# Prompt attention's two-map weights scaled, subtracted and turned by TensorE products with diagonals from ScalarE, in place of VectorE arithmetic and a transpose

## What is computed

```python
def diff_attn_prompt(q, k, v, lam):
    ...
    def block(args):
        qi, i = args
        s = jnp.einsum('bqhmd,bkhmd->bhmqk', qi, k, preferred_element_type=F32) * ATTN_SCALE
        qpos = i * Q_BLOCK + jnp.arange(Q_BLOCK)
        s = jnp.where(kpos[None, :] <= qpos[:, None], s, -jnp.inf)
        p = jax.nn.softmax(s, axis=-1)
        w = p[:, :, 0] - lam * p[:, :, 1]
        return jnp.einsum('bhqk,bkhd->bqhd', w.astype(v.dtype), v)
```

## Time and profile before

| what | value |
|---|---|
| median of 3 runs | 2125.33 us (2123.13 to 2126.2) |
| the profiled execution | 2127.41 us, its span 2125.8 us |
| mean granted clock of TensorE over the span | 0.916 |
| TensorE busy | 1877.3 us, 88% of the span |
| VectorE busy | 780.2 us, 37% |
| ScalarE busy | 722.0 us, 34% |
| GpSimd busy | 174.3 us, 8% |
| the chain that ended last | TensorE 72%, transfers 8%, SyncE's queue 5%, VectorE 4%, ScalarE 3% |

### The profile page before, as it was taken

One profiled execution on the slowest core, in us unless ns is written; L12 is line 12 of the kernel. 1 busy time (PEld: TensorE's weight loads), 2 busy tenths in 40 slices (PEclk: granted clock), 3 DMA queues, 4 the chain that ended last, 5 costly groups with the idle time before them and its releaser, 6 DMA issues.

```text
span 2125.8 us, 43188 instructions
## 1 busy us (share of the span) xinstructions
PE 1877.3 (88%) x17058; PEld 1647.2 (77%) x17058; DVE 780.2 (37%) x1200; ACT 722.0 (34%) x1056; POOL 174.3 (8%) x321
## 2 busy tenths in 40 slices
PE   4999995999999978979878988788769599999998
PEld 1647994999999978977433767677539599999997
DVE  3993333333322333156477222222223423333222
ACT  4432333333332223244333644344111333333222
POOL 2100122000000221010010000000004200000000
PEclk9899996999999988989677999999768799999999
DMA  8775321222222221212442899899851122222222
GB/s 233 261 265 177 95 86 30 79 84 84 79 68 81 82 86 50 79 50 90 133 134 90 272 393 349 322 345 381 318 186 50 35 84 79 85 83 67 82 81 72
DMA packets 245680, 302.86 MB, mean 142 GB/s; under 512 B 10451, under 2 KB 195774, under 8 KB 245438
## 3 DMA queue, kind: packets, MB, share of 16 engines
q1 hardware_dynamic: 241504, 292.14, 41.6%
q10 hardware_dynamic: 3142, 8.11, 1.1%
q0 software_dynamic: 928, 1.06, 0.2%
HBM read 293.89 MB, written 7.37 MB: 142 GB/s over the span
## 4 chain that ended last, share of the span: by engine, by line
PE 72%; DMA 8%; SPq 5%; DVE 4%; issue 4%; ACT 3%; POOL 2%; DVEq 0%; POOLq 0%; ACTq 0%
PE ps L538 54%; PE ps L464 5%; DMA kpg<-in_cache_k 4%; SPq L415 3%; PE ps L491 2%; SPq L422 2%; PE ps L778 1%; DMA vpg<-in_cache_v 1%; PE ps L829 1%; PE ps L926 1%; PE ps L815 1%; DMA xcm<-in_x_sample 1%; PE ps L684 1%; PE ps L767 1%; PE ps L677 1%
## 5 line engine op out<-in xcount | busy, mean ns | idle before, releaser
L538 PE MATMUL ps<-hr,ws 128*128 128x288 f32 x5760 | 796.7, 301 | 60.4 <-DVE hr L1838 60.4
L538 PEld LDWEIGHTS ps<-hr,ws 128*128 128x128 f32 x5760 | 787.9, 193 | 70.3 <-issue 37.4
L1832 DVE TENSOR_TENSOR ws<-raw,ws 128x1024 fp32r<-128x1024 f32 x200 | 234.8, 1175 | 715.4 <-ACT ws L1219 715.4
L1219 ACT ACTIVATE ws<-raw 128x1024 fp32r<-128x1024 f32 x200 | 201.5, 1009 | 709.6 <-PE ps L538 651.9
L538 PE MATMUL ps<-gr,ws 128*128 128x288 f32 x2112 | 281.9, 296 | 0.0
L538 PEld LDWEIGHTS ps<-gr,ws 128*128 128x128 f32 x2112 | 281.7, 189 | 0.0
L1399 ACT ACTIVATE kTs<-ps 128x512 f32<-128x512 f32 x256 | 140.0, 596 | 184.5 <-PE ps L464 184.3
L464 PE MATMUL ps<-identz,kpg 128*128 128x128 f32 x1024 | 147.3, 291 | 35.1 <-DMA kpg<-in_cache_k 33.8
L464 PEld LDWEIGHTS ps<-identz,kpg 128*128 128x128 f32 x1024 | 119.7, 149 | 59.5 <-ACT kTs L1399 29.5
L491 PE MATMUL ps<-raw,cond 128*32 128x256 f32 x896 | 87.5, 484 | 28.8 <-DMA raw<-in_w_ada_mix 23.3
L538 PE MATMUL ps<-hg,ws 128*128 128x288 f32 x768 | 104.1, 299 | 3.1 <-DVE mark L1825 3.1
(11 more groups left out here) (320 smaller groups left out, 1588.9 us busy)
## 6 DMA issues: line engine op xcount, KB each, us to landing
kpg<-in_cache_k SPq DMA_DIRECT2D x128, 512.0 KB, 5.8
vpg<-in_cache_v SPq DMA_DIRECT2D x128, 512.0 KB, 5.9
raw<-in_ffn_w SPq DMA_DIRECT2D x88, 512.0 KB, 3.8
raw<-in_w_ada_mix SPq DMA_DIRECT2D x48, 512.0 KB, 5.2
raw<-in_w_ada_ffn SPq DMA_DIRECT2D x48, 512.0 KB, 4.3
raw<-in_ffn_w SPq DMA_DIRECT2D x48, 384.0 KB, 3.3
raw<-in_w_ada_kv SPq DMA_DIRECT2D x16, 512.0 KB, 4.9
raw<-in_ssm_w_glu SPq DMA_DIRECT2D x16, 512.0 KB, 4.1
```

The costliest lines, as they stand in the source:

```text
L538: last = mm(ps[:, 4 * s + 2 * tile + h, 0:HALF], ws[:, wslot, w, k, :], src[:, k0 + k, v, h * HALF:(h + 1) * HALF], start=first, stop=(end ...
L1219: A(ws[:, w, 0, 0:nk, :].rearrange("p k n -> p (k n)"), raw[:, slot, 0:nk, :].rearrange("p k n -> p (k n)"), ACT.Copy).then_inc(slab_high, 1)
L1832: TT(f(ws[:, w, 1, 0:nk, :]), f(raw[:, slot, 0:nk, :]), f(ws[:, w, 0, 0:nk, :]).bitcast(F32), ALU.subtract).then_inc(raw_done[slot], 1)
```

## The change

VectorE's `block_weights` ends after the reciprocal and the factor of minus lambda. ScalarE gets a new step, `block_diag`, after the exponentials of the following block: it waits for w_done and writes two 128x128 diagonal matrices (the identity times the two per-query factors) into a new buffer `diag`, of two parities; semaphore d_done. TensorE's `block_weights` waits for d_done instead of w_done and makes, for each 128 keys, two matmuls that accumulate in PSUM: exponentials of map 0 turned by the first diagonal, plus those of map 1 turned by the second. These give the scaled, subtracted and turned weights in one go.

```diff
-    l01 = share("l01", [P, 2, 8], 46 * KB)
+    l01 = share("l01", [P, 2, 8], 47 * KB)
...
+    diag = share("diag", [P, 2, 2, P], 44 * KB + 512)
...
             def block_weights(h, i):
-                pe.wait_ge(w_done, h * QB + (i + 1))
+                pe.wait_ge(d_done, h * QB + (i + 1))
                 pe.wait_ge(wp_copied, h * QB + (i + 1))
                 for k in range(i + 1):
-                    last = turn(ps[:, 4 + i % 2, k * P:(k + 1) * P], e01[:, i % 2, 0, k * P:(k + 1) * P])
+                    for m in range(2):
+                        last = mm(ps[:, 4 + i % 2, k * P:(k + 1) * P], e01[:, i % 2, m, k * P:(k + 1) * P], diag[:, i % 2, m, :],
+                                  start=(m == 0), stop=(m == 1))
                 last.then_inc(wp_turned, 1)
...
+            def block_diag(h, i):
+                act.wait_ge(w_done, h * QB + (i + 1))
+                for m in range(2):
+                    done = A(diag[:, i % 2, m, :], ident, ACT.Copy, scale=l01[:, i % 2, 6 + m:7 + m])
+                done.then_inc(d_done, 1)
...
                         elif not (final and hp):
                             block_exp(h + 1, 0)
+                        block_diag(h, i)
                         if i == 1 and not (first and hp == 0):
                             head_output(h - 1)
...
             def block_weights(h, i):
 
-                w, par = (i + 1) * P, i % 2
-                l_, e0, e1 = l01[:, par], e01[:, par, 0, 0:w], e01[:, par, 1, 0:w]
+                l_ = l01[:, i % 2]
                 dve.wait_ge(e_done, h * QB + (i + 3))
                 step(REC(l_[:, 6:8], l_[:, 4:6]))
-                step(TT(l_[:, 7:8], l_[:, 7:8], neglam[:, :], ALU.mult))
-                step(TS(e1, e1, l_[:, 7:8], None, ALU.mult))
-                STT(e0, e0, l_[:, 6:7], e1, ALU.mult, ALU.add).then_inc(w_done, 1)
+                TT(l_[:, 7:8], l_[:, 7:8], neglam[:, :], ALU.mult).then_inc(w_done, 1)
```

More of the change, by code:

```diff
@@ L247, in yoco_step @@
     tri = share("tri", [P, P], 44 * KB)
+    diag = share("diag", [P, 2, 2, P], 44 * KB + 512)
+    assert 44 * KB + 512 + 4 * 4 * P <= 47 * KB
     kpg = share("kpg", [P, 4, H, P], 0)
@@ L305, in yoco_step @@
         picks_ready, sums_done, sums_root, sums_inv, spread = sems("picks_ready sums_done sums_root sums_inv spread")
-        head_in, s_full, s_max, e_done, w_done, wp_turned, wp_copied, pv_full, head_out = sems(
-            "head_in s_full s_max e_done w_done wp_turned wp_copied pv_full head_out")
+        head_in, s_full, s_max, e_done, w_done, d_done, wp_turned, wp_copied, pv_full, head_out = sems(
+            "head_in s_full s_max e_done w_done d_done wp_turned wp_copied pv_full head_out")
         k_full, v_full = [sem(f"k_full{s}") for s in range(4)], [sem(f"v_full{s}") for s in range(4)]
@@ L1981, in _ @@
             head_pair(0, first=True)
-            with step.loop(1, H // 2 - 2, 2 * QB * 5) as k:
+            with step.loop(1, H // 2 - 2, 2 * QB * 3) as k:
                 head_pair(k)
```

## The result

The changed kernel takes **2136.45 us** (median of 5 runs, 2135.32 to 2141.02) against 2125.33 in the same series (5 runs, 2119.41 to 2128.91): a ratio of 1.0062, 95% interval 1.0040 to 1.0084. It is slower by 11 us. The profiled execution took 2141.02, its span 2139.4.

A forecast was written before the change was run, and what follows sets the result against it. TensorE's ring in prompt attention, waiting for VectorE's scaled weights, was taken as the bound. A pair of heads grows from 30.5 to 33.6 us, times 3.5 pairs +11 us on 2125.3: 2136, range 2128 to 2143.

The forecast's parts named there:

- The removal: Prompt attention, VectorE: dropping L1955 (12.4 us) and L1956 (17.6 us) can by itself win at most 30 us.
- the ring: Prompt attention's chain of waits between engines over 32 blocks, returning to TensorE: 15.25 us a head, 30.5 a pair before.
- The diagonals: ScalarE, behind the next block's exponentials: two 128x128 writes cost 0.68 us a pair, bounds 0.45 and 0.81.
- The waits: TensorE's waits: 2.10 us ahead of block 2, 0.28 and 0.85 ahead of block 3, 1.14 at the second head's end.
- The walk: Step-by-step timing of two heads at full clock: 31.8 us a pair, 25.3 of work and 6.5 of waiting.
- The clock: TensorE in prompt attention: a tenth of the work at half clock in place of 30%, giving 33.6 us a pair.
- ScalarE is never late: Rival: TensorE finds each diagonal ready, leaving 25.3 us of work a pair; -18 us, 2107; chance 0.04.
- S+3.10: First head: block 3's exponentials start on ScalarE 3.10 us after S, the start of block 3's scores on TensorE.
- full clock throughout: Rival: TensorE stays at full clock because bursts are longer; 31.8 us a pair, +4.5, 2130; chance 0.21.
- The clock falls as often as now: Rival: 30% of TensorE's work stays at half clock; 37.9 us a pair, +26, 2151; chance 0.07.
- No change: Rival: diagonal writes cost 0.45 us a pair and the clock holds; 30.7 a pair of heads, 2126; chance 0.08.
- The prediction's own sign against the rule: Trace before: from 1169.43 TensorE did sixteen transposes for 3.69 us at half clock, then the clock rose to full.

The follow-up runs named there:

- e4_no_vector: Kernel before, with VectorE's scaling of map 1 and subtraction left out, TensorE turning map 0's bare exponentials: 2098.58 us.
- e9_transposes: Changed kernel with its 160 products put back to 80 transposes of map 0's exponentials, still waiting for the diagonals; scales and second map left out: 2126.23 us.
- e8_no_link: Changed kernel without ScalarE's diagonal step; TensorE's products take both maps against the identity and wait for VectorE's scales: 2109.97 us.
- e1_early: Changed kernel with VectorE's scales ahead of the next block's reduction and ScalarE's diagonals ahead of the next block's exponentials: 2110.0 us, ratio 0.9933.
- e2_products: Kernel before, with each transpose of a block of weights made twice as a full-precision product with the identity, no diagonals: 2121.06 us.

## Why the prediction was right

The forecast was 2136 in a range of 2128 to 2143; 2136.45 was measured. The mechanism held; two terms were off and cancelled, and the bound on the removal held by luck.

- **The removal.** VectorE's 30 us were called the most that the removal could win. Alone it shortens the stretch by 27.9 (e4_no_vector), but only 11.5 of that is less idle time of TensorE; 16.4 is its clock, for which the bound had no term although the prediction itself counts 5.6 us a pair of work done at half clock. That the two stayed under 30 together was luck.
- **What takes it back.** In the stretch: 114.8 before; 86.9 without VectorE's part; 115.4 with the link too (+28.5, e9_transposes); 125.6 with the products too (+10.2). "So the change removes VectorE's link of the ring and puts ScalarE's in its place, equally late, and TensorE's longer groups come on top" was the sentence; taken in this order the link eats the whole gain, and the loss that is left is the groups. The shares depend on the order in which the parts are added: with the products first (e8_no_link, 100.7) they cost 13.8 and the link 24.9.
- **The diagonals.** Priced at 0.68 a pair from L1088; the timeline shows 0.68 and 0.69, one of them 395 ns. The Trainium skill, "ScalarE: Activation LUTs", What ACT_TABLE_LOAD costs, gives 186 ns and 0.833 a column for an activation with immediate scale and bias, 93 more for an operand read from a per-partition pointer, and an overlap of 93 between neighbours: an estimate of 386 ns for one and 0.68 us for the pair, and the trace agrees.
- **The waits.** 2.10 ahead of block 2, measured 1.97; 0.28 and 0.85 ahead of block 3, measured 0.33 and 0.90 in the pair of heads at full clock; 1.14 ahead of the next head's block 0, measured 0.96. These measured waits begin when the scores ahead of them are wholly done, 0.07 us later than in the walk (0.49 in the profile for the narrowest scores, which it counts as 0.42).
- **The walk.** 31.8 us a pair at full clock. The widest reductions of the changed kernel, with the next two heads at full clock, start at

```profile
1059.09 1.22 DVE L1956 TENSOR_REDUCE l<-ps 128x2 f32<-128x1024 f32 x1
1074.81 1.22 DVE L1956 TENSOR_REDUCE l<-ps 128x2 f32<-128x1024 f32 x1
1091.35 1.22 DVE L1956 TENSOR_REDUCE l<-ps 128x2 f32<-128x1024 f32 x1
```

15.72 and 16.54, 32.26 for the pair: **0.46 short**. Nearly all of it is the groups, counted from start to start as in the walk: at full clock (e1_early's timeline) groups of 4, 8, 12 and 16 records take 0.65, 1.09, 1.54 and 1.89, or 5.17 a head where I had 4.96. My 0.14 for a group's start was a little low.
- **The clock.** A tenth of the work at half clock was to cost 1.8 a pair net. Over all seven heads the widest reductions are 117.4 us apart (1059.09 to 1176.52), 33.55 a pair, so it cost 1.3. That term was too dear by 0.5 and the walk too cheap by 0.46: the 33.6 came out right by two errors that cancel. That the clock would stay above 0.73 and between 0.85 and 0.95 held (0.87 in the window of the earlier trace rows, 1038 to 1170).
- **Not held:** that everything outside the stage stays as long as it was. In the profiles the stage began 8 us later, and what lies behind the last head's values took 6 less (951.1 against 957.1). Neither can be put down to the change: the start of the stage moves by as much between kernels that are alike up to there, and the part behind it takes 947.2 to 955.0 in the eleven other profiles, though its code is the same. That the widest reductions would be 16 to 17.5 us apart held for their mean, 16.8, and for two of the seven gaps; the others are 15.72 (three times), 17.75 and 18.99.

Of the rivals, "ScalarE is never late" had nearly the right price for a thing that needed one more edit, the order of both engines. I put 25.3 us a pair and 2107 on it; e1_early and e8_no_link, where TensorE hardly waits ahead of the products, run a pair in 26.3 and 26.4 and take 2110. I bound its condition to ScalarE's order as the diff has it (start of the exponentials at S+3.10), and there it fails. What I did not ask is what ScalarE does before S+3.10: nothing, for 2.40 us. The rival "full clock throughout" is refuted: the clock in the stretch is 0.92, and the products of block 2 at 1111.88 above run near half clock (2.81 us, granted clock 0.53, against 1.60 at full for the same group at 1062.63). "The clock falls as often as now" would have kept it near the 0.76 of before. "No change" needed a pair of diagonals in 0.45 us; it takes 0.68.

## What to carry to other kernels

Where a change puts an engine's new step into a ring, look at what that engine does right before the step: a short step that stands behind a long wait costs the ring as much as the work it replaced, and ahead of that wait it costs nothing (25 us of a 125 us stretch here), if what the step needs is made early enough too. Effects in a ring don't add: price a removal with the new link in place, since whatever is late next decides what the removal is worth. And measure a stage by its own landmarks where its start moves by more than the effect.

## What was not expected of the hardware

**In these runs the clock went with the waits and the length of the groups between them, not with the kind of instruction.** With the same 80 transposes the granted clock in the stretch was 0.92 where TensorE waited 8.7 us (e4_no_vector) and 0.76 where it waited 25.9 (e9_transposes). With 22 us of waits and four times the records it was 0.92 for products and 0.90 for transposes. The Trainium skill, "TensorE: Matmul & The Clock Gate", Part 4: PE-mode transpose, says that transposes don't engage the full clock; the runs here differ from it: with 320 transposes in the stage, 49.7 us of TensorE's time, the clock in the stretch was 0.90. No run has a stage of transposes alone. The prediction's own sign against the rule was weaker, as 4.65 us of values ended 0.7 us before its sixteen transposes.

**A wait costs more than its length.** The link adds 13.7 us of idle time to TensorE's 80 transposes, and 14.8 us of busy time for the same instructions (e4_no_vector to e9_transposes, clock 0.92 to 0.76). With the products it adds 18.5 of idle time and 6.4 of busy time (e8_no_link to the changed kernel, 0.96 to 0.92). Idle time alone does not set the clock: e2_products was idle for 12.9 us at 0.97.

**The start of the stage moves by 14 us** (1038.6 to 1052.4) between profiles of kernels that are the same up to there, more than the change is worth. Why is open; no run was made for it.
